# RMSNorm factor taken behind the matmuls, and two-half difference scores, in a two-layer diffusion backbone

## What is computed

```
for i in range(DEPTH):
    h  = h + 0.5 * m[2] * swiglu(modulate(rmsnorm(h, ffn1_norm[i]), m[0], m[1]), w1, w3, w2)     # hc likewise, with mc
    n_lat = modulate(rmsnorm(h, mix_norm[i]), m[3], m[4])                                        # n_ctx likewise
    p = n @ w_in[i]          # pooling | multi-head latent attention | differential attention
    c = (softmax(q1 k1^T) - lam * softmax(q2 k2^T)) v                # 4 heads, 64 wide each
    h  = h + m[5] * (concat(a, b, c) @ w_out[i])
    h  = h + 0.5 * m[8] * swiglu(modulate(rmsnorm(h, ffn2_norm[i]), m[6], m[7]), w1, w3, w2)
return rmsnorm(h, final_norm)
rmsnorm(x, g) = x * rsqrt(mean(x*x) + eps) * g;  modulate(n, shift, scale) = n * (1 + scale) + shift
swiglu(x) = (silu(x @ w1) * (x @ w3)) @ w2
```

## Time and profile before

| | |
|---|---|
| median of 3 runs (lowest, highest) | 3138.59 us (3137.93, 3139.87) |
| the profiled execution | 3136.8 us |
| its span, first to last instruction | 3134.9 us |
| busy: TensorE, VectorE, ScalarE, GpSimd | 94%, 49%, 28%, 3% of the span |
| mean granted TensorE clock | 0.975 |

### The profile page before, as it was taken

How to read it: one execution, slowest core, us unless ns; L and a number is a source line. 1 busy time by engine, 2 the same in 40 slices (tenths; PEclk the granted TensorE clock), 3 DMA queues, 4 the chain that set the end, 5 groups by cost and what they waited for, 6 DMA issues and landing times.

```text
span 3134.9 us, 40610 instructions
## 1 busy us (share of the span) xinstructions
PE 2957.6 (94%) x15626; PEld 2440.8 (78%) x15626; DVE 1538.9 (49%) x2496; ACT 874.9 (28%) x1174; POOL 108.5 (3%) x82
## 2 busy tenths in 40 slices
PE   7999999989879889999999899999989879899998
PEld 3888888878657578888888788888868647678886
DVE  4666565631476447655666423422342376443333
ACT  3221122121346622211221321122131246432222
POOL 0000000000430000000000000000000230000000
PEclk9999999999899899999999999999999999999999
DMA  5434344322200023443443123222213200123332
GB/s 190 127 114 136 107 127 124 91 54 61 53 1 1 4 71 107 127 125 105 118 135 100 47 60 100 82 60 60 70 45 81 60 1 1 57 78 105 90 101 73
DMA packets 422143, 254.64 MB, mean 81 GB/s; under 512 B 25921, under 2 KB 417705, under 8 KB 422058
## 3 DMA queue, kind: packets, MB, share of 16 engines
q1 hardware_dynamic: 422058, 253.48, 27.5%
HBM read 251.35 MB, written 2.10 MB: 81 GB/s over the span
## 4 chain that ended last, share of the span: by engine, by line
PE 86%; DVE 6%; ACT 4%; issue 2%; DMA 0%; SPq 0%; ACTq 0%; DVEq 0%
PE pair L569 77%; PE pair L675 3%; PE pair L747 2%; PE pair L696 1%; PE pair L503 1%; PE pair L679 1%; DVE buf L1127 1%; ACT buf L961 1%; DVE n_lo L1118 1%; ACT L834 1%; DVE mod_acc L1183 1%; DVE proj L1255 1%; PE pair L658 1%; DVE buf L1254 1%; ACT L837 0%
## 5 line engine op out<-in xcount | busy, mean ns | idle before, releaser
L569 PE MATMUL pair<-n_hi,hi_w 128*128 128x512 f32 (+1 forms) x3224 | 903.5, 350 | 57.3 <-DVE n_lo L1118 42.7
L569 PE MATMUL pair<-n_lo,hi_w 128*128 128x512 f32 (+1 forms) x3224 | 901.8, 349 | 0.0
L569 PE MATMUL pair<-n_hi,lo_w 128*128 128x512 f32 (+1 forms) x3224 | 897.5, 347 | 0.0
L569 PEld LDWEIGHTS pair<-n_hi,hi_w 128*128 128x128 f32 x3224 | 515.2, 190 | 143.7 <-issue 51.8
L1074 DVE TENSOR_TENSOR lo_w<-raw_w,hi_w 128x1024 fp32r<-128x1024 f32 (+1 forms) x296 | 386.2, 1305 | 438.7 <-ACT hi_w L815 435.2
L569 PEld LDWEIGHTS pair<-n_lo,hi_w 128*128 128x128 f32 x3224 | 518.6, 190 | 82.8 <-issue 0.2
L569 PEld LDWEIGHTS pair<-n_hi,lo_w 128*128 128x128 f32 x3224 | 515.6, 189 | 82.1
L815 ACT CAST hi_w<-raw_w 128x1024 fp32r<-128x1024 f32 (+1 forms) x296 | 328.9, 1112 | 395.2 <-PE pair L569 390.2
L1183 DVE SCALAR_TENSOR_TENSOR mod_acc<-mod_w,silu_c,mod_acc 128x256 f32<-128x256 f32 x896 | 360.4, 482 | 0.0
L569 PE MATMUL pair<-h_hi,hi_w 128*128 128x512 f32 x1232 | 341.4, 347 | 2.2 <-DVE lo_w L1074 2.2
L569 PE MATMUL pair<-h_lo,hi_w 128*128 128x512 f32 x1232 | 341.3, 346 | 0.0
(11 more groups left out here) (158 smaller groups left out, 1835.0 us busy)
## 6 DMA issues: line engine op xcount, KB each, us to landing
raw_w<-in_ffn_w SPq DMA_DIRECT2D x176, 512.0 KB, 3.8
mod_w<-in_w_mod SPq DMA_DIRECT2D x64, 1024.0 KB, 5.1
raw_w<-in_ffn_w SPq DMA_DIRECT2D x64, 704.0 KB, 4.7
raw_w<-in_w_in SPq DMA_DIRECT2D x38, 512.0 KB, 3.9
pro_w<-in_w_mod SPq DMA_DIRECT2D x2, 4096.0 KB, 18.2
raw_w<-in_w_out SPq DMA_DIRECT2D x16, 512.0 KB, 4.1
x_tok<-in_x SPq DMA_DIRECT2D x4, 512.0 KB, 5.8
out<-x_tok SPq DMA_DIRECT2D x4, 512.0 KB, 2.7
```

Of the source, the lines that this page charges most:

```text
L569: mm = pe.matmul(pair[s][:, a:a + m], wt[:, k * P:(k + 1) * P], tile(src, k, m, a), start=(n == 0 and wt is hi and src is src_hi), stop=(n ...
```

## The change

The rstd factor is no longer part of n_hi and n_lo. They now hold x * scale (`high` and `low`), and each activation tile gets two more columns in front, the shift for the latents and the shift for the context (`NT = TOK + 2`). The matmul of these two columns gives the product of weights and shift; behind the matmul VectorE multiplies the result by rstd and copies the two columns out (`bias`), and ScalarE adds the bias (with SiLU in slot 0 of an up sweep). A pass over 768 tokens is now 512 and 258 columns, and one over 512 tokens 258 and 256 (`streams`).

At three of the six norms (layer 0 input, layer 1 FFN1, layer 1 input) `high` and `low` run inside the sweep that ends the step before, tile by tile as x is updated; TensorE's sums follow slot 0 of the first unit. At the other three (`late_rows`: the very first one, and FFN2 in both layers) they run at the norm, both slots of the first unit go together, and in FFN2 the sums stand behind the fifth tile of that unit.

The masked key copies are gone; the two difference scores are matmuls over 64 rows, one on each half of the partitions, issued in turn (`scores_diff`), both behind the exponentials of both maps. The diff, cut to its core:

```
+def late_rows(w):
+    return w["base"] == 0 or w["what"] == "ffn2_up"
...
+def ntile(tensor, k, n=TOK, at=0):
+    return tensor[:, bass.ds(k * NT + 2 + at, n)]
+def streams(w, s):
+    return ((0, 512, 0), (512, NT - 512, 512)) if w["ctx"][s] else ((0, 258, 254), (258, 256, 512))
+def first_col(w, s):
+    return 0 if w["ctx"][s] else 254
+def shift_cols(tensor):
+    return tensor[:, :].rearrange("p (k c) -> p k c", c=NT)[:, :, 0:2]
+def norm_of(w):
+    L = w["layer"]
+    chunk, gain = {"ffn1_up": (0, G_FFN1), "in": (3, G_MIX), "ffn2_up": (6, G_FFN2)}[w["what"]]
+    return mod_col(L, chunk), L * G_LAYER + gain
...
-    def unit(w, i, slots, first):
+    def unit(w, i, slots, first, sums=0):
...
+                if n == 0:
+                    pe.wait_ge(shift_ready, cnt["n"] // KD + 1)
                 pe.wait_ge(n_ready, cnt["n"] + k + 1)
             for s in slots:
                 hi, lo = hi_w[s], lo_w[s]
                 for wt, src in ((hi, src_hi), (hi, src_lo), (lo, src_hi)):
-                    for a, m in halves(width(w, s)):
-                        mm = pe.matmul(pair[s][:, a:a + m], wt[:, k * P:(k + 1) * P], tile(src, k, m, a),
-                                       start=(n == 0 and wt is hi and src is src_hi),
-                                       stop=(n == w["kt"] - 1 and wt is lo))
+                    opens, closes = n == 0 and wt is hi and src is src_hi, n == w["kt"] - 1 and wt is lo
+                    if down or w["what"] == "out":
+                        for a, m in halves(width(w, s)):
+                            mm = pe.matmul(pair[s][:, a:a + m], wt[:, k * P:(k + 1) * P], tile(src, k, m, a),
+                                           start=opens, stop=closes)
+                    else:
+                        for a, m, at in streams(w, s):
+                            mm = pe.matmul(pair[s][:, at:at + m], wt[:, k * P:(k + 1) * P],
+                                           src[:, k * NT + a:k * NT + a + m], start=opens, stop=closes)
                 if n == w["kt"] - 1:
                     mm.then_inc(unit_done[s], 1)
+            if sums and n == 4:
+                sum_stream(sums)
...
-        if starts_norm(w):
-            unit(w, 0, (0, 1), True)
+        both = starts_norm(w) and late_rows(w)
+        if both:
+            unit(w, 0, (0, 1), True, norm_width(w) if w["base"] else 0)
         else:
             unit(w, 0, (0,), True)
+        if starts_norm(w) and not both:
+            sum_stream(norm_width(w))
         if before is not None and mod_tile(before) is not None:
             mod_fold(before)
-        if not starts_norm(w):
+        if not both:
...
+        def scores_diff(h, q0, k0, nk):
+            for s in range(2):
+                if cnt["s"][s]:
+                    pe.wait_ge(exp_done[s], cnt["s"][s])
+                cnt["s"][s] += 1
+            for a, m in halves(nk):
+                for s in range(2):
+                    rows_s = slice(DDIM * s, DDIM * (s + 1))
+                    mm = pe.matmul(pair[s][:, a:a + m], tile(proj, T_DQ + h, P, q0)[rows_s, :],
+                                   tile(proj, T_DK + h, m, k0 + a)[rows_s, :], start=True, stop=True)
+                    if a + m == nk:
+                        mm.then_inc(s_ready[s], 1)
...
+    def shift_high(w):
+        act.wait_ge(scale_ready, cnt["n"] // KD + 1)
+        shift, _ = norm_of(w)
+        act.copy(shift_cols(n_hi), mod[:, shift:shift + 2 * KD].rearrange("p (k e) -> p k e", e=2))\
+           .then_inc(shift_hi, 1)
+    def high(k, w_cols):
+        act.wait_ge(scale_ready, cnt["n"] // KD + 1)
+        for e, (a, m) in enumerate(halves(w_cols)):
+            ins = act.activation(ntile(n_hi, k, m, a), tile(x, k, m, a), ACT.Identity,
+                                 scale=scale_a[:, bass.ds(2 * k + e, 1)])
+        ins.then_inc(nhi_ready, 1)
+    def norm_x(w_cols, w):
         if w is not None:
             split_hi(w, 0, 1, True)
+            if late_rows(w) and w["base"]:
+                before = [v for v in SWEEPS if v["layer"] == w["layer"] and v["what"] == "out"][0]
+                for s in range(2):
+                    act.wait_ge(unit_done[s], before["base"] + before["n"])
+                    act.wait_ge(pair_free[s], before["base"] + before["n"])
+                shift_high(w)
+                for k in range(KD):
+                    high(k, w_cols)
+                cnt["n"] += KD
         cnt["x"] += 1
         act.wait_ge(xsum_done, cnt["x"])
         std(pair[3], w_cols, D)
-        if shift is None:
-            return
-        if cnt["n"] == 0:
+        cnt["used"] = None
+        if w is not None and w["base"] == 0:
             act.wait_ge(mrow_done, 1)
             act.copy(mod_rows[0:2, 0:D], pair[0][0:2, :]).then_inc(mrow_out[0], 1)
-        for k in range(KD):
-            act.wait_ge(t_ready, cnt["n"] + k + 1)
-            for e, (a, m) in enumerate(halves(w_cols)):
-                ins = act.activation(tile(n_hi, k, m, a), buf[k % 2][:, a:a + m], ACT.Identity,
-                                     bias=mod[:, shift + 2 * k + e:shift + 2 * k + e + 1])
-            ins.then_inc(nhi_ready, 1)
-        cnt["n"] += KD
-        cnt["used"] = (t_ready, cnt["n"])
+            shift_high(w)
+            for k in range(KD):
+                high(k, w_cols)
+            cnt["n"] += KD
...
         if what.endswith("_up"):
             if s == 0:
-                act.wait_ge(unit_done[0], n)
-                if not (isinstance(n, int) and n == 1):
-                    act.wait_ge(pair_free[1], n - 1)
-                act.activation(act_buf[:, 0:width(w, 0)], pair[0][:, 0:width(w, 0)], ACT.Silu)\
-                   .then_inc(pair_free[0], 1)
+                act.wait_ge(pair_free[0], n)
+                for e, (a, m) in parts:
+                    ins = act.activation(act_buf[:, a:a + m], act_buf[:, a:a + m], ACT.Silu,
+                                         bias=bias[0][:, e:e + 1])
+                ins.then_inc(silu_done, 1)
             else:
-                act.wait_ge(pair_free[1], n)
+                act.wait_ge(hid_ready, cnt["h"] + i + 1)
                 act.copy(tile(h_hi, i, width(w, 1)), hid_buf[:, 0:width(w, 1)]).then_inc(hhi_ready, 1)
         elif ends_step(w):
             act.wait_ge(pair_free[s], n)
+            if w["to"] is not None and not late_rows(w["to"]):
+                high(2 * i + s, norm_width(w["to"]))
             square_x(i, s, width(w, s))
-        elif what == "in" and s == 0:
-            act.wait_ge(unit_done[0], n)
-            act.activation(tile(proj, w["arg"] + 2 * i, width(w, 0)), pair[0][:, 0:width(w, 0)], ACT.Identity,
-                           scale=SC_DIFF if w["arg"] == T_DQ else 1.0).then_inc(pair_free[0], 1)
+        elif what == "in":
+            act.wait_ge(pair_free[s], n)
+            act.wait_ge(std_ready, cnt["std"])
+            for e, (a, m) in parts:
+                to = tile(proj, w["arg"] + 2 * i + s, m, a)
+                ins = act.activation(to, to, ACT.Identity, bias=bias[s][:, e:e + 1],
+                                     scale=SC_DIFF if w["arg"] == T_DQ else 1.0)
+            ins.then_inc(in_done[s], 1)
...
+    def low(k, w_cols):
+        dve.wait_ge(nhi_ready, cnt["n"] + k + 1)
+        for e, (a, m) in enumerate(halves(w_cols)):
+            ins = dve.scalar_tensor_tensor(out=ntile(n_lo, k, m, a), in0=tile(x, k, m, a),
+                                           scalar=scale_a[:, bass.ds(2 * k + e, 1)],
+                                           in1=ntile(n_hi, k, m, a).bitcast(F32), op0=ALU.mult, op1=ALU.subtract)
+        ins.then_inc(n_ready, 1)
...
+            scales(w)
         cnt["x"] += 1
         split_lo(w, 0, 1)
+        if late_rows(w):
+            shift_low(w)
+            for k in range(KD):
+                low(k, w_cols)
+            cnt["n"] += KD
         wait_rstd()
-        def low(k):
-            dve.wait_ge(nhi_ready, cnt["n"] + k + 1)
-            for e, (a, m) in parts:
-                ins = dve.scalar_tensor_tensor(out=tile(n_lo, k, m, a), in0=buf[k % 2][:, a:a + m],
-                                               scalar=mod[:, shift + 2 * k + e:shift + 2 * k + e + 1],
-                                               in1=tile(n_hi, k, m, a).bitcast(F32), op0=ALU.add, op1=ALU.subtract)
-            ins.then_inc(n_ready, 1)
-        for k in range(KD):
-            if k >= 2:
-                dve.wait_ge(n_ready, cnt["n"] + k - 1)
-            for e, (a, m) in parts:
-                ins = dve.scalar_tensor_tensor(out=buf[k % 2][:, a:a + m], in0=tile(x, k, m, a),
-                                               scalar=scale_a[:, 2 * k + e:2 * k + e + 1],
-                                               in1=rstd[:, a:a + m], op0=ALU.mult, op1=ALU.mult)
-            ins.then_inc(t_ready, 1)
...
     def finish(w, i, s):
         n, what = w["base"] + i + 1, w["what"]
+        m_all, c0 = width(w, s), first_col(w, s)
         if what.endswith("_up"):
```

(47 more changed lines are left out.)

133 lines of the change are left out of this document (72 added, 61 removed).

## The result

The changed kernel takes 3155.9 us (median of 5) against 3138.6 (median of 5 beside it): ratio 1.0057, 95% interval 1.0042 to 1.0072, so it is slower by 17.3 us. The prediction was 3141 with a range of 3120 to 3170: the time lies in the range. It had given 0.42 to slower and 0.58 to faster or no change, and 3155.9 is above the 3128 to 3154 over which its own small errors were to spread it. The profiled execution has a span of 3154.1 us against 3134.9, +19.2. The page after, part 1, answers to the earlier trace rows: TensorE has 5.4 us more work, VectorE 145 us more.

What follows compares the result with a forecast made beforehand. The prediction took TensorE, busy 94% of the span, as the bound: its own work and the waits before it, most at the norms. Its terms summed to +2.1 us on the 3138.6 us median, giving 3141 us, range 3120 to 3170.

Steps and rivals of the forecast that it cites:

- Ahead norms: Layer 0 input, layer 1 FFN1 and input: high and low made in the sweep before shorten TensorE's waits, -41.9 us.
- Late norms: First norm and both FFN2 norms, where x is not ready ahead: -1.5, +2.1 with 0.5 slow clock, -0.4; sum +0.7 us.
- Layer 0's first units: Start of layer 0's two second-group up sweeps: TensorE waits about 3.1 us, plus 1.6 slow clock, twice: +9.4 us.
- Steady loop: Layer 0's up sweeps: low-half loop 16.8 us against TensorE's unit of 16.9, some 40 units; +2.0 us, bounds 0 and +20.
- the down sweeps: Layer 0's two last down sweeps: high stands in front of square and cast, delaying the first unit; with clock +3.7 us.
- Rival D: Layer 0's loop exceeds TensorE's 16.9 us unit; at 0.5 us more over 40 units, 3159 us; chance 0.12.
- Moving columns: Up and input sweeps: two more columns in 768-column passes, +3.3 us; 512-column passes split at 17 ns each, +20.0 us.
- rival E: Split passes: fixed 15.7 ns not paid again by the second half, 5 ns for 17; about 3125 us; chance 0.18.
- Rival C: Short matmuls bound by their weight loads: 266 ns per split pass, +43 instead of +20, 3164 us; chance 0.09.
- Difference scores: Mixer's 40 steps: row halves overlap; circle from scores through both exponentials 4.6 to 4.8 us a step, +3.0 us.
- mixer: Last input unit finished in two operations, +1.2 us per layer; ScalarE's 16 key splits go, worth 0.5; +1.9 us in all.
- rival B: Difference scores: two row halves run one behind the other, first score 0.85 us later; +29 instead of +3, 3167 us; chance 0.17.

Runs made afterwards that it cites:

- ahead only: Late factor kept only for the three norms made ahead, the other three norms, their sweeps and the difference scores as in the kernel before: 3109.9 us, ratio 0.9912.
- plain last: The norms first kernel with layer 1's FFN2 norm and sweeps as in the kernel before, no split passes there: 3125.4 us, ratio 0.9962.
- own waits: The ahead only kernel with 64-row scores, each map's two matmuls behind its own wait, first map ahead of second: 3110.9 us, ratio 0.9908.
- scores alone: The kernel before with the new 64-row difference scores, without key splits and mask: 3149.6 us, ratio 1.0032.
- norms alone: The changed kernel with the old full-row difference scores, key splits and mask: 3138.7 us, ratio 1.0003.
- first unit: The changed kernel with the first unit's product taken before the modulation sums in layer 0's two second-group up sweeps: 3149.2 us, ratio 1.0034.
- norms first: The changed kernel with old difference scores and the first unit's product taken ahead of the modulation sums: 3133.3 us, ratio 0.9991.
- pairs on that base: The ahead only kernel with its old scores replaced by the new 64-row difference scores: 3119.2 us, ratio 0.9937.
- padded kernel: The kernel before with one satisfied TensorE wait repeated four times in the prologue, moving later instructions: 3138.5 us, ratio 0.9997.

## Why the prediction was right and wrong

**Ahead norms, -41.9.** Measured -39.9. Right, mechanism and size.

**Late norms, +0.7.** Measured -1.8 (the first -2.9). Right within its reach; the point that they gain nothing was right.

**Layer 0's first units, +9.4.** The wait was right (2.91 for 3.1 us) and its undoing gave 5 to 7 us with its clock. **Steady loop, +2.0, and the down sweeps, +3.7.** Here the ledger has some 12 us more than forecast in layer 0's FFNs. The sum took cover for granted to 0.1 us: the low halves of a steady unit come every 17.05 or 17.31 us in turn, against 16.96 before, and passes are slower too. Rival D is thus in part true (+0.1 to +0.3 per unit). Giving the old sweeps back to layer 0 (ahead only against plain last) is worth 15.5 us.

**Moving columns, +3.3 and +20.0.** Both mis-sized, and nearly even in sum, which is luck: the split costs 6.7 ns, and 9.8 in the changed kernel, instead of 17, between forecast and rival E, and the two columns 2.8 instead of 0.8. Rival C (266 ns) is refuted. The Trainium skill, page "TensorE: Matmul & The Clock Gate", section "Back-to-back issue gap", gives 2.5 ns beside the columns for an isolated matmul; the 6.7 ns measured for one more matmul in a pass agree with neither it nor my 15.7. What stood wrong in the step was that the excess of a single 512-column stream over its columns is not a price per matmul.

**Difference scores, +3.0, and mixer, +1.9.** This step failed. The circle was right and rival B's serial halves were refuted (4.63 us at 2.4 GHz), but I took the circle at the full clock for all 40 steps. Its first term is the score pair, and at the 1.2 GHz with which both stages begin it is 2.93 us, not 1.50: by my own circle 6.0 us, which the trace has. The old order hid the second map there (4.9 to 5.1). Those steps also leave TensorE busy for half the time (2.93 of 6.00 us), and the clock comes back about two steps later. The mixer's own term was of the right size: from the last input matmul to the first maximum the trace has +1.9 and +0.5 us in the two layers. Measured for the scores: +10.0 alone, +9.2 on the other base. "TensorE's gain is not on the circle" was true: work taken from an engine without shortening the circle is idle time. That the idle time then holds the clock down is seen in the later return of 2.4 GHz (909 against 899); the falls in later windows (0.86) came in some traces and not in others with as much idle time or more, and what decides them stays open. The Trainium skill, page "TensorEngine Tiling (Array Packing)", section "Key Properties", says that a change of tiling mode drains TensorE. In the pairs' steps such a drain could hide in the 0.93 us of idle time. Where TensorE is full, with own waits, transposes and value products take 2.14 us (2560.34 to 2562.48) where the earlier trace rows have 2.00 (2564.85 to 2566.85), so I estimate 0.14 us a step at most; no run separates it.

```profile
2560.34 0.87 PE L777 MATMUL pair<-ident,buf 128*128 128x128 f32 x6
...
2562.48 2.25 PE L751 MATMUL pair<-proj 64*128 64x512 f32 x8
...
2564.66 0.87 PE L777 MATMUL pair<-ident,buf 128*128 128x128 f32 x6
```

**Sum.** For the norms part alone my terms give -0.4, measured +0.9 (-2.5 to +4.1); for the scores alone +2.5, measured +10.0 (+5.3 to +14.8). The remaining 7 us between these and the +17.9 of both (13.2 to 22.6) may be nothing. But the scores cost 17.2 and 15.9 us in the two kernels that keep the late factor everywhere (the changed kernel against norms alone, first unit against norms first), and 9 to 10 in the two others. The traces point to the untouched down sweeps: norms alone has 91.53 us for 528 matmuls (346.7 ns per pass), the changed kernel 93.28 (353.3). Over all down sweeps the two pairs of traces are 11.2 and 11.0 us apart; scores alone against before, and the two on the "ahead only" base, 1.4 at most. The pairs on that base have 91.53 us as well, so it isn't the 64-row matmuls that slow those passes; as in the padded kernel, the rate goes with the program, and why stays open.

That the time lay in the range is in part luck: the range was 50 us wide, and the misses (scores and layer 0's FFNs above, moving columns below the forecast) partly cancel.

```profile
1946.08 91.53 PE pair L618 x528
```

## What to carry to other kernels

When two results are made at once instead of one behind the other, write the loop down twice, at both levels of the clock, and from the stage's first step: a circle that is even at full clock can lose where the stage starts slow, and the freed engine may stay slow for longer. Keep each result behind its own wait: 64-row scores in the old order gave steps of 4.32 us where the old had 4.58 and the pairs 4.63, though the whole kernel was no faster for it (ratio 0.9908 against 0.9912). And take a factor out of the operand only where the operand can then be made ahead; elsewhere it bought nothing here, and its price per pass stays. And a few us in one trace prove little: moving the program alone changed single sweeps by 2 us and more.
